# Alternating the two token tiles' PSUM banks inside each weight unit, with the low-part products last

## The reference

```
h = rms_norm(x);  z = h @ w_in                       # 6656 columns
A = grouped-query attention with axial rotary        # 8 heads
B = three dilated window attentions, combined by softmax denominators
C = multi-scale mean pooling, per-group linear map
x = x + (sigmoid gates * [A @ wa, B @ wb, C @ wc] summed) @ w_out
h2 = rms_norm(x)
x = x + (silu(h2 @ w_gate) * (h2 @ w_up)) @ w_down   # inner width 2816
```

## Time and profile before

| what | value |
|---|---|
| time of three runs | 900.97, 901.82, 903.81 us; median 901.82 us |
| span of the profiled execution | 901.1 us |
| TensorE busy | 883.2 us, 98% of the span, 4156 matmuls and transposes |
| VectorE busy | 541.8 us, 60% |
| ScalarE busy | 420.6 us, 47% |
| granted TensorE clock, mean | 0.997 |
| weight stream | 136 loads of 1024 KB |

### The profile page before, as it was taken

How to read it: one execution, slowest core, us unless ns; L and a number is a source line. 1 busy time by engine, 2 the same in 40 slices (tenths; PEclk the granted TensorE clock), 3 DMA queues, 4 the chain that set the end, 5 groups by cost and what they waited for, 6 DMA issues and landing times.

```text
span 901.1 us, 11409 instructions
## 1 busy us (share of the span) xinstructions
PE 883.2 (98%) x4156; PEld 720.5 (80%) x4156; DVE 541.8 (60%) x608; ACT 420.6 (47%) x506; POOL 74.1 (8%) x89
## 2 busy tenths in 40 slices
PE   4999999999999999999999999999999999999998
PEld 3887888888888888888868778888888888888886
DVE  3899344554866666654468974445468766666542
ACT  5665544346444544443447555343554444444330
POOL 2442000000003000000022320000000200000000
PEclk9999999999999999999999999999999999999999
DMA  8554333333446554555545433242344555555551
GB/s 322 220 179 153 140 109 142 111 152 141 171 171 217 186 188 184 186 187 187 188 146 193 177 141 140 105 160 109 140 148 180 187 204 187 187 187 187 180 177 64
DMA packets 22441, 151.73 MB, mean 168 GB/s; under 512 B 2624, under 2 KB 2800, under 8 KB 4848
## 3 DMA queue, kind: packets, MB, share of 16 engines
q1 hardware_dynamic: 20576, 144.25, 44.1%
q0 software_dynamic: 1808, 6.72, 2.3%
HBM read 149.91 MB, written 1.05 MB: 168 GB/s over the span
## 4 chain that ended last, share of the span: by engine, by line
PE 96%; DMA 2%; issue 1%; DVE 0%; SPq 0%; ACT 0%; DVEq 0%; ACTq 0%
PE bank L860 28%; PE bank L862 27%; PE bank L871 27%; PE bank L891 5%; PE bank L995 4%; PE bank L976 2%; PE bank L964 2%; DMA w_raw<-in_stream_dram 2%; PE bank L941 1%; PE bank L970 0%; PE bank L947 0%; DVE w_lo L612 0%; SPq L373 0%; DVE aT_lo L639 0%; DVE x_sb L768 0%
## 5 line engine op out<-in xcount | busy, mean ns | idle before, releaser
L606 DVE TENSOR_TENSOR w_lo<-w_raw,w_hi 128x2048 fp32r<-128x2048 f32 x134 | 306.5, 2290 | 116.3 <-ACT w_hi L471 115.8
L860 PE MATMUL bank<-w_hi,aT_hi 128*128 128x512 f32 x832 | 335.3, 403 | 7.9 <-ACT w_hi L467 4.0
L862 PE MATMUL bank<-w_hi,aT_lo 128*128 128x512 f32 x832 | 326.7, 393 | 0.0
L471 ACT ACTIVATE w_hi<-w_raw 128x2048 fp32r<-128x2048 f32 x134 | 256.0, 1911 | 91.4 <-DMA w_raw<-in_stream_dram 91.4
L871 PE MATMUL bank<-w_lo,aT_hi 128*128 128x512 f32 x832 | 224.6, 391 | 0.7 <-DVE w_lo L612 0.3
L860 PEld LDWEIGHTS bank<-w_hi,aT_hi 128*128 128x128 f32 x832 | 157.4, 189 | 41.5 <-issue 6.7
L871 PEld LDWEIGHTS bank<-w_lo,aT_hi 128*128 128x128 f32 x832 | 155.8, 188 | 34.8 <-DVE w_lo L612 1.8
L862 PEld LDWEIGHTS bank<-w_hi,aT_lo 128*128 128x128 f32 x832 | 157.7, 189 | 30.8
L860 PE MATMUL bank<-w_hi,hT_hi 128*128 128x512 f32 x176 | 69.9, 397 | 0.0
L862 PE MATMUL bank<-w_hi,hT_lo 128*128 128x512 f32 x176 | 69.6, 395 | 0.0
L716 DVE TENSOR_REDUCE neg_max<-bank 128x2 f32<-128x512 f32 (+1 forms) x32 | 22.1, 691 | 67.9 <-PE bank L976 38.2
(11 more groups left out here) (99 smaller groups left out, 760.4 us busy)
## 6 DMA issues: line engine op xcount, KB each, us to landing
w_raw<-in_stream_dram SPq DMA_DIRECT2D x136, 1024.0 KB, 4.8
bias_sb<-in_b_gate_dram POOLq DMA_DIRECT2D x12, 256.0 KB, 5.0
par<-in_params_dram POOLq DMA_DIRECT2D x3, 384.0 KB, 3.6
pool_mat<-in_pooling_dram POOLq DMA_DIRECT2D x1, 1024.0 KB, 7.5
out_dram<-x_sb SPq DMA_DIRECT2D x4, 256.0 KB, 4.1
x_sb<-in_x_dram SPq DMA_DIRECT2D x1, 512.0 KB, 4.7
x_sb<-in_x_dram POOLq DMA_DIRECT2D x1, 512.0 KB, 7.3
gates<-in_mask_dram POOLq DMA_DIRECT2D x1, 512.0 KB, 13.7
```

Source lines behind the costliest of these rows:

```text
L471: nc.scalar.activation(w_hi[:, j % RING, :, :].rearrange("p k n -> p (k n)"), w_raw[:, j % RING, :, :].rearrange("p k n -> p (k n)"), ACT. ...
L606: nc.vector.tensor_tensor(w[0], w[1], w[2].bitcast(F32), ALU.subtract).then_inc(unit_lo, 1)
L860: nc.tensor.matmul(o, src[0][:, k, tok], w_hi[:, slot, wk + i, :], start=first and i == 0, stop=False)
L862: nc.tensor.matmul(o, src[1][:, k, tok], w_hi[:, slot, wk + i, :], start=False, stop=False)
```

## The change: what it does

`rows` is gone and `columns` does both tiles. For each slice `k` it issues act_hi for tile 0, act_hi for tile 1, act_lo for tile 0, act_lo for tile 1, so each matmul goes to the other bank than the one before. All 16 matmuls with `w_hi` come first, then every turn of `turns_within(t)` in whatever unit, then the wait for `w_lo` and the 8 matmuls with it, again alternating. The wait for a free bank (`wait_free`) is done for both tiles ahead of the unit's first matmul. No instruction of another engine is changed, and the number of matmuls is the same.

```
             def columns(lay, t, name, src, tiles, first, final, wk=0):
+                opening, slot = wk == 0, t % RING
+                outs = [B((name, m))[:, :] for m in range(MT)]
+                toks = [slice(P * m, P * m + P) for m in range(MT)]
                 if first:
-                    wait_free(pe, lay, (name, m))
+                    for m in range(MT):
+                        wait_free(pe, lay, (name, m))
                 if opening and t:
                     pe.wait_ge(unit_hi, lay * (UNITS - 1) + t)
                 for i, k in enumerate(tiles):
                     if opening and not t:
                         pe.wait_ge(first_hi, lay * UK + (i + 1))
-                    nc.tensor.matmul(o, src[0][:, k, tok], w_hi[:, slot, wk + i, :], start=first and i == 0,
-                                     stop=False)
-                    nc.tensor.matmul(o, src[1][:, k, tok], w_hi[:, slot, wk + i, :], start=False, stop=False)
-                if opening and t in TURNS_FIRST:
+                    for a in src:
+                        for m in range(MT):
+                            nc.tensor.matmul(outs[m], a[:, k, toks[m]], w_hi[:, slot, wk + i, :],
+                                             start=first and i == 0 and a is src[0], stop=False)
+                if opening:
                     for turn in turns_within(t):
                         transposes(lay, turn)
...
-                    last = nc.tensor.matmul(o, src[0][:, k, tok], w_lo[:, slot, wk + i, :], start=False,
-                                            stop=final and i == len(tiles) - 1)
-                if final:
-                    full(last, (name, m))
+                    closing = final and i == len(tiles) - 1
+                    for m in range(MT):
+                        last = nc.tensor.matmul(outs[m], src[0][:, k, toks[m]], w_lo[:, slot, wk + i, :],
+                                                start=False, stop=closing)
+                        if closing:
+                            full(last, (name, m))
                 return last
-
-            def columns(lay, t, name, src, tiles, first, final, wk=0):
-                rows(lay, t, name, 0, src, tiles, wk, first, final, opening=wk == 0)
-                if wk == 0 and t not in TURNS_FIRST:
-                    for turn in turns_within(t):
-                        transposes(lay, turn)
-                return rows(lay, t, name, 1, src, tiles, wk, first, final)
```

More of the change, by code:

```diff
@@ L846, in _, with columns @@
             pe.sem_inc(unit_done, RING)
-            def rows(lay, t, name, m, src, tiles, wk, first, final, opening=False):
-                tok = slice(P * m, P * m + P)
-                o, slot = B((name, m))[:, :], t % RING
+            def columns(lay, t, name, src, tiles, first, final, wk=0):
+                opening, slot = wk == 0, t % RING
+                outs = [B((name, m))[:, :] for m in range(MT)]
+                toks = [slice(P * m, P * m + P) for m in range(MT)]
                 if first:
-                    wait_free(pe, lay, (name, m))
+                    for m in range(MT):
+                        wait_free(pe, lay, (name, m))
                 if opening and t:
```

## The result

| | before | after |
|---|---|---|
| runs, median | 901.39 us (4 runs, 900.94 to 903.81) | 905.96 us (4 runs, 904.56 to 906.43) |
| ratio | | 1.0041, 95% interval 1.0028 to 1.0055 |
| span of the profiled execution | 901.1 us | 903.8 us |

A forecast was written before the change was run, and what follows sets the result against it. It took TensorE's 512-column matmuls, 0.226 us each and 82% of the chain, as the bound. Terms 2.8 + 0 + 0.7 = +3.5 us on 901.8 gave 905.3 us; range 901.2 to 909, likeliest case 903.7 to 907.5.

The forecast's parts named there:

- The distance from start to start: All 512-column matmuls: changing bank each time is neither cheaper nor dearer than staying, so 3264 alternations cost 0.
- what is loaded as weights: Matmuls on aT against hT: the start-to-start distance follows the operand loaded as weights, not which bank is written.
- The low products last: Every unit: the low part is needed 1.8 us later, but nearly all have slack already, so this buys nothing there.
- Layer 1, unit 0: Start of layer 1: possible gain of 1.6 us lost to a later VectorE chain; taken at 0, bounds -1.6 and +0.6.
- The swap of waits: Start of layer 1: TensorE's wait for w_lo becomes a wait for the turn's low parts at unit 1.
- the add's delay: Before layer 1's unit 0: D1's last add ends at 456.7 instead of 456.31, moving VectorE's chain by 0.4 us.
- Layer 0, unit 0: Start of layer 0: the 2.5 us wait stays, since ScalarE does the turns only behind unit 2's split; 0.
- The FFN turns: Units 34 to 36: 2.70 us of cover for 3.5 of work; +1.4 us a layer, +2.8 in all.
- `merged` in unit 30: Turns `merged` 0 and 1: two steps take 2.6 us against 2.8 of cover; 0, up to +0.5 a layer.
- rival 3: Banks come free late and each of 14 boundaries stalls, at 0.5 us each +7, so 912 us; chance 0.12.
- The end: End of kernel: last two adds run one after the other, +0.4, and the store adds 0.3; +0.7 us (0.4 to 2.3).
- Rival 2: Turns' stall is smaller or unit 0 gives 1.6 us back; total within 2.7 us, about 903 us; chance 0.30.

The follow-up runs named there:

- experiments 1: The changed kernel with the turns of units 0, 30, 34 and 35 back behind 8 matmuls: 902.21 us, ratio 0.9998 to the kernel before.
- experiment 3: Against the kernel before: tile by tile without alternation, low products last, those four units' turns behind 8 matmuls: 902.15 us, ratio 0.9997.
- experiment 7: The kernel before with hT and the mixer's tiles allocated right behind aT_lo, lower in SBUF: 899.91 us, ratio 0.9965.
- experiment 4: The changed kernel with the last unit of each layer tile by tile as before: 905.71 us, ratio 1.0040 to the kernel before.
- experiment 8: Tile by tile, low products last, ScalarE's unit 0 turns ahead of unit 2's split: 897.90 us, ratio 0.9950 to before; with hT lower too: 896.06 us, 0.9925.

## Why the prediction was right

**The distance from start to start (taken at 0).** Right. 0.2267 us on `aT` and 0.2334 on `hT` before and after, and in experiments 1 and 3. Whether the bank changes 24 times in a unit or once makes no difference.

**What the distance follows.** The prediction's "what is loaded as weights" was argued from two rows; experiment 7 shows it for `hT`, and makes it narrower: the place of that tile, not its content. The Trainium skill's 215.7 ns (TensorE: Matmul & The Clock Gate, section "Wait — 56ns, not 53.3ns?") was reached by none of these kernels; 226.7 is the lowest mean here.

**The low products last (no gain from slack).** Right. No unit waited for w_lo after the change, and the one wait that went was replaced.

**Layer 1, unit 0 (taken at 0).** The swap of waits came as described. In the trace the unit gave 0.4 us back: it starts 0.55 us later after the jump and is 0.9 shorter. The step that failed is the add's delay: the second add does end 0.4 us later, but the first piece of w_lo does not start later for it (experiment 4).

**Layer 0, unit 0 (0).** Right in kind: the same wait is there (2.4 us). Unit 1 started 0.45 us earlier, counted from the first matmul, and unit 2 another 0.17. But the kernel of experiment 4, which has the changed kernel's layer 0, gives 0.1 for unit 1, and that of experiment 7, which has the old order there, gives 0.3. So single executions of the same layer 0 differ here by 0.3 to 0.4 us, and the 0.45 can't be put down to the change. Perhaps the first loads arrive differently, which no run separates.

**The FFN turns (2.8 us).** The mechanism and its price are what the runs show: a chain of 3.54 us (3.5 forecast) with a cover of only 2.7, gone behind 8 or 12 matmuls, back in the kernel before when only the turns move. The term was mis-sized: 3.4 us, not 2.8. The missing part is the restart. After each stall the first distance is 0.33 us and some of the next are 0.228 to 0.236 before 0.227 returns: 0.11 us more at unit 35 of layer 1, 0.15 at unit 36.

**`merged` in unit 30 (0, bound 0.5 a layer).** 0.28 us a layer, inside the bound, but not nothing. The two steps were forecast at 2.6 us and took 2.88, against a cover of 2.75 (2.8 forecast). Unit 31 starts 0.15 us late, and a stall that short pays the restart as well, which makes unit 32 later by 0.12 to 0.14.

**Banks (rival 3).** Right: 1.1 us of slack forecast, 1.1 read. That more cover is there at the other boundaries was not measured, but TensorE's list of waits has no wait on them, and no unit from 3 to 30 has a step of 0.1 us in either layer. The Trainium skill's rule (Perfetto Trace Analysis, section "Optimizing Tensor Performance"), that one group's evacuation should overlap the next group's matmuls, showed at the end of the kernel alone.

**The end (0.7 us).** 0.5 us: the second add's 0.4 as forecast, and 0.1 and not 0.3 for the store.

**Sum.** 3.4 (FFN turns) + 0.6 (`merged`) + 0.5 (the end) - 0.4 (layer 1's unit 0) = 4.1 us from the trace. Less layer 0's units 0 and 1 (0.6) and a first matmul that came 0.7 us earlier, it is 2.8, which is the difference of the two spans (903.8 - 901.1 = 2.7) to a tenth. The ratio says 3.7 us (2.5 to 5.0); 3.5 was forecast. The mechanism and the largest term were right. That the total came so close is partly luck: the two terms of the turns came 1.2 us above the forecast, and the end and layer 1's unit 0 0.6 us below.

**Rival 2 (within 2.7 us).** Both of its grounds failed: the stall was larger than forecast, not smaller, and unit 0 gave back 0.4 us, not 1.6. The interval of the ratio alone, from 2.5 us, would not quite exclude it.

## What to carry to other kernels

When matmuls are put in another order, first measure the distance from start to start across the boundary that the new order will multiply; here two rows of the old trace already said that a change of bank is free. Then look at what else stands in the reordered list: transposes that feed another engine's chain must keep a cover, in matmuls behind them, that is longer than the chain, and their place is a decision of its own. Here the chain was 3.54 us: 12 matmuls behind the eight transposes were enough (3.6 us), and 8 were not (2.7). The order of matmuls was worth nothing here; a wait on ScalarE's list and a tile's address were worth about 3.2 us each by their ratios.

## What the runs showed of the hardware

**The place of the stationary tile in SBUF sets the distance.** fp32r matmuls of 512 columns start every 226.7 ns with `aT` and every 233.4 ns with `hT`; `hT` moved down by some 76 KB a partition, by the sizes of the tiles allocated ahead of it, runs at 226.7 (experiment 7). `oT` and `mixT`, which lie behind `par` in all kernels, stay at 234. Where the border lies was not looked for.

**A short gap can halve the clock for a stretch, or not.** In the kernel before, a gap of 2.5 us in layer 0 was followed by 3.4 us at half clock, which cost 1.7 us more; in experiment 3's profiled execution a gap of 2.8 us at the same place was followed by the full clock (window, length, TensorE, and so on; granted clock 1.00):

```profile
23.50:27.00 3.50, 3.42 (x15) 2.85 (x16) 3.50 (x2) 3.41 (x7) 1.72 (x2) 1.00 0.44 183
```

In experiment 4 the gap ahead of layer 1 was followed by half clock too. So 1.7 us of difference between two single executions of these kernels may mean nothing but this; in both kernels of experiment 8, too, the gap of the jump was followed by half clock. Of the eight profiled kernels that have layer 0's gap, six show it there; of all eleven, three show it behind the jump.

**A stall costs more than its length.** After a wait TensorE's first distance is 0.33 us and not 0.227, and most of the next two to eight are 0.228 to 0.236, 0.11 to 0.15 us more in all (the changed kernel, units 31, 35 and 36 of layer 1). Behind the eight transposes of unit 34 the first distance is 0.31 us, with no wait there.
